# The last two hidden chunks of each MLP stage share one accumulation per token tile

## What is computed

```python
def swiglu(h, w_gu, w_down):
    g, u = jnp.split(h @ w_gu, 2, axis=-1)
    return (jax.nn.silu(g) * u) @ w_down

def _sq_relu_mlp(h, w1, w2):
    return jnp.square(jax.nn.relu(h @ w1)) @ w2

def sandwich(x, fn, g_pre, g_post, shift, scale, gate, res_w):
    h = modulate(rmsnorm(x, g_pre), shift, scale)
    y = rmsnorm(fn(h), g_post)
    return x + res_w * gate[:, None, :] * y
...
    x = sandwich(x, ffn1, ...)      # 2816 hidden columns
    x = sandwich(x, mix, ...)
    x = sandwich(x, ffn2, ...)      # 2816 hidden columns
...
        x = x + gx1 * _rms_norm(_token_mixer(h, kv_ctx, rope, lp, lam, lam_init), g_post_mix[l])
        hm = _modulate(x, g_pre_mlp[l], sx2, cx2)
        x = x + gx2 * _rms_norm(_sq_relu_mlp(hm, w_ff1[l], w_ff2[l]), g_post_mlp[l])   # 4096 hidden columns
```

## Time and profile before

| | us |
|---|---|
| runs (3) | 4396.05, 4403.17, 4407.77 |
| median | 4403.17 |
| the profiled execution | 4407.63 |
| its span | 4405.6 |

### The profile page before, as it was taken

How to read it: one execution, slowest core, us unless ns; L and a number is a source line. 1 busy time by engine, 2 the same in 40 slices (tenths; PEclk the granted TensorE clock), 3 DMA queues, 4 the chain that set the end, 5 groups by cost and what they waited for, 6 DMA issues and landing times.

```text
span 4405.6 us, 50811 instructions
## 1 busy us (share of the span) xinstructions
PE 3956.6 (90%) x18628; PEld 3175.8 (72%) x18628; DVE 2291.0 (52%) x3495; ACT 1369.2 (31%) x1832; POOL 1346.1 (31%) x1012
## 2 busy tenths in 40 slices
PE   7999899989997979789879879999787989788999
PEld 6888676867776748558668768888674747577887
DVE  4676844146664361641682367777445353834334
ACT  3222633242224242252112331111424243225223
POOL 2444332434432103003222223322220303434443
PEclk8999999999998989899989989999998999899999
DMA  4454221233331102001111123332110201222222
GB/s 180 176 190 156 85 72 63 96 115 128 137 132 49 39 0 72 20 1 58 57 58 58 58 82 125 118 119 100 45 48 10 82 1 67 77 84 79 95 95 86
DMA packets 57219, 364.66 MB, mean 83 GB/s; under 512 B 5744, under 2 KB 12144, under 8 KB 13936
## 3 DMA queue, kind: packets, MB, share of 16 engines
q1 hardware_dynamic: 42064, 271.11, 17.5%
q10 hardware_dynamic: 15008, 91.49, 5.5%
HBM read 360.49 MB, written 2.10 MB: 82 GB/s over the span
## 4 chain that ended last, share of the span: by engine, by line
issue 66%; POOL 23%; PE 10%; DVE 0%; ACT 0%; POOLq 0%; DVEq 0%; ACTq 0%
POOL b_wlo L561 23%; PE ps L1647 3%; PE ps L1648 3%; PE ps L1649 3%; POOLq L575 0%; ACT ps L616 0%; DVE b_y L1156 0%; DVE b_x L1160 0%; PE ps L1699 0%; DVE b_y L1183 0%; PE ps L1710 0%; ACT b_whi L602 0%; POOLq L577 0%; DVE b_y L1209 0%; PE ps L1723 0%
## 5 line engine op out<-in xcount | busy, mean ns | idle before, releaser
L561 POOL TENSOR_TENSOR b_wlo<-b_raw,b_whi 128x512 fp32r<-128x512 f32 x1008 | 1345.9, 1366 | 3039.1 <-ACT b_whi L602 3039.1
L1647 PE MATMUL ps<-b_hhi,b_whi 128*128 128x512 f32 (+1 forms) x3160 | 1178.5, 373 | 69.5 <-DVE b_vp L1548 28.8
L1648 PE MATMUL ps<-b_hlo,b_whi 128*128 128x512 f32 (+1 forms) x3160 | 1163.3, 368 | 0.0
L1649 PE MATMUL ps<-b_hhi,b_wlo 128*128 128x512 f32 (+1 forms) x3160 | 1161.4, 368 | 0.0
L1647 PEld LDWEIGHTS ps<-b_hhi,b_whi 128*128 128x128 f32 x3160 | 603.5, 191 | 177.2 <-issue 57.3
L602 ACT ACTIVATE b_whi<-b_raw 128x2048 fp32r<-128x2048 f32 x252 | 480.7, 1908 | 752.4 <-PE ps L1649 744.9
L1648 PEld LDWEIGHTS ps<-b_hlo,b_whi 128*128 128x128 f32 x3160 | 603.7, 191 | 97.8 <-issue 2.2
L1649 PEld LDWEIGHTS ps<-b_hhi,b_wlo 128*128 128x128 f32 x3160 | 602.2, 191 | 99.1
L1104 DVE SCALAR_TENSOR_TENSOR b_macc<-b_mraw,b_csil,b_macc 128x256 f32<-128x256 f32 x868 | 506.0, 639 | 7.0
L1209 DVE TENSOR_TENSOR b_y<-ps,b_y 128x512 f32<-128x512 f32 x496 | 335.8, 689 | 274.7 <-PE ps L1649 274.7
L1647 PE MATMUL ps<-b_whi,b_dhi 128*128 128x512 f32 x992 | 399.7, 403 | 53.5 <-POOL b_wlo L561 29.0
(11 more groups left out here) (277 smaller groups left out, 4752.0 us busy)
## 6 DMA issues: line engine op xcount, KB each, us to landing
b_raw<-panels SPq DMA_DIRECT2D x252, 1024.0 KB, 4.8
b_mraw<-mod_panels ACTq DMA_DIRECT2D x78, 1024.0 KB, 6.7
b_y<-mod_panels ACTq DMA_DIRECT2D x3, 1024.0 KB, 15.9
b_xin<-xT SPq DMA_DIRECT2D x1, 2048.0 KB, 25.5
b_mraw<-mod_panels SPq DMA_DIRECT2D x2, 1024.0 KB, 19.0
b_rope<-rope ACTq DMA_DIRECT2D x4, 512.0 KB, 3.9
outT<-b_xout SPq DMA_DIRECT2D x4, 512.0 KB, 3.8
b_mod<-mod_panels ACTq DMA_DIRECT2D x1, 1024.0 KB, 20.9
```

Of the source, the lines that this page charges most:

```text
L561: ins = pool.tensor_tensor(wlo[:, s, c], raw[:, s, c], whi[:, s, c].bitcast(F32), ALU.subtract)
L1647: pe.matmul(out, a[0], b[0], start=first, stop=False)
L1648: pe.matmul(out, a[0], b[1], start=False, stop=False)
L1649: return pe.matmul(out, a[1], b[0], start=False, stop=last)
```

## The change

`last_downs` takes the place of the last two rounds. It makes the parts of chunk C-2 for output tiles 0, 1 and 2, then the modulation sums of the last chunk, and then, for every output tile, the part of chunk C-1 into the same bank without clearing it (from tile 3 on preceded by the part of chunk C-2). DVE adds each tile once. The last chunk's work leaves the loop (ffn1 and ffn2 run one trip less and have one chunk more ahead of it); the number of modulation sums per chunk stays. D0 and D1 are both released only in the last output tile. N0 is split after the root of the last post step, where N1 was; N1 after the last pre root, ahead of the norm's tail. The low part of a padding panel at the very end is dropped.

```diff
-    MLPS = {"ffn1": Mlp("ffn1", True, L, first["ffn1"], 8, ((2, 2), 3, 4)),
-            "ffn2": Mlp("ffn2", True, L, first["ffn2"], 36, ((), 2, 5)),
+    MLPS = {"ffn1": Mlp("ffn1", True, L, first["ffn1"], 8, ((2, 2, 3), 3, 3, (3,))),
+            "ffn2": Mlp("ffn2", True, L, first["ffn2"], 36, ((2,), 2, 4, (2,))),
...
-            upto = next_panel(st) + 1 if st in NEXT else n_panels
+            upto = next_panel(st) + 1 if st in NEXT else MLPS["mlp2"].p0 + 2 * MLPS["mlp2"].C
...
                     if t == last and pre:
-                        split(next_panel(st) + 1)
+                        split(next_panel(st))
+                        if finish:
+                            split(next_panel(st) + 1)
...
+            if pre:
+                split(next_panel(st) + 1)
             norm_tail(st)
...
-            split(m.p0 + m.UP * m.C + m.C)
             gate_rows(AFTER[st], (0, 1, 2, 3))
...
             for c in m.rest:
-                units(c)
-                for o in range(O):
-                    add(c - 1, o)
+                units(c, mods=m.rest_mods(c))
+                if c < m.C - 1:
+                    for o in range(O):
+                        add(c - 1, o)
             prepare(AFTER[st])
             def finish(t):
-                add(m.C - 1, 2 * t)
-                add(m.C - 1, 2 * t + 1)
+                add(m.C - 2, 2 * t)
+                add(m.C - 2, 2 * t + 1)
...
+            def last_downs():
+                p, c = m.panel(m.C - 1) + m.UP, m.C - 2
+                def part(o, n):
+                    tok, half = slice(o // 2 * P, (o // 2 + 1) * P), o % 2
+                    if n == 0:
+                        prior = O * (c + 1) + o - 3 if o >= 3 else O * c + max(q for q in range(O) if q % 3 == o)
+                        pe.wait_ge(*at("added", ("start", st), prior + 1))
+                    for k in range(2):
+                        ins = tri(ps[:, 4 + o % 3, :], (dhi[:, (c + n) % 2, k, tok], dlo[:, (c + n) % 2, k, tok]),
+                                  wtile(p + n, 2, D, k, half * 512, 512), n == k == 0, n == k == 1)
+                    if o == O - 1:
+                        ins.then_inc(panel_used, 1)
+                    elif n == 1:
+                        ins.then_inc(*up("down"))
+                pe.wait_ge(lo_ready, p + 1)
+                pe.wait_ge(*at("hid_lo", ("start", st), 2 * c + 2))
+                for o in range(3):
+                    part(o, 0)
+                sums(m.rest_mods(m.C - 1))
+                pe.wait_ge(lo_ready, p + 2)
+                pe.wait_ge(*at("hid_lo", ("start", st), 2 * c + 4))
+                for o in range(O):
+                    if o >= 3:
+                        part(o, 0)
+                    part(o, 1)
+                    if o == 1:
+                        gate_rows(AFTER[st], (0, 1, 2, 3))
...
-            down(m.C - 1, m.p0 + (m.UP + 1) * m.C - 1)
+            last_downs()
```

More of the change, by code:

```diff
@@ L233, in __init__ @@
         self.O = 2 * T // P
-        self.lead, self.half, self.trips = mods
+        self.lead, self.half, self.trips, self.tail = mods
         self.loop0 = 1 + len(self.lead)
         self.rest = range(self.loop0 + 2 * self.trips, self.C)
+        assert len(self.tail) == len(self.rest) >= 1
         self.per_trip = 2 * (self.UP + 1)
@@ L251, in loop_mods, with rest_mods @@
         return self.mod0 + sum(self.lead) + u * self.half, self.half
+    def rest_mods(self, c):
+        n = c - self.rest[0]
+        return self.mod0 + sum(self.lead) + 2 * self.trips * self.half + sum(self.tail[:n]), self.tail[n]
 class Rows:
@@ L461, in program @@
     first = {**{n: 10 ** 6 for n in ("mix1", "ffn2", "mix2", "mlp1", "mix3", "mlp2")}, **first}
-    MLPS = {"ffn1": Mlp("ffn1", True, L, first["ffn1"], 8, ((2, 2), 3, 4)),
-            "ffn2": Mlp("ffn2", True, L, first["ffn2"], 36, ((), 2, 5)),
-            "mlp1": Mlp("mlp1", False, TT, first["mlp1"], 56, ((), 2, 7)),
-            "mlp2": Mlp("mlp2", False, L, first["mlp2"], 84, ((), 0, 7))}
+    MLPS = {"ffn1": Mlp("ffn1", True, L, first["ffn1"], 8, ((2, 2, 3), 3, 3, (3,))),
+            "ffn2": Mlp("ffn2", True, L, first["ffn2"], 36, ((2,), 2, 4, (2,))),
+            "mlp1": Mlp("mlp1", False, TT, first["mlp1"], 56, ((), 2, 7, (0,))),
+            "mlp2": Mlp("mlp2", False, L, first["mlp2"], 84, ((), 0, 7, (0,)))}
     LAYER, TOKENS = {"mix2": 0, "mix3": 1}, {"mix2": TT, "mix3": L}
@@ L708, in mlp @@
             for c in m.rest:
-                units(c, m.panel(c))
+                units(c, m.panel(c), mods=m.rest_mods(c))
                 split(m.panel(c) + m.UP + 1)
-            split(m.p0 + m.UP * m.C + m.C)
             gate_rows(AFTER[st], (0, 1, 2, 3))
@@ L1205, in add @@
                 else:
-                    dve.wait_ge(panel_used, lin(down_panel(m, c) + 1, m.per_trip, i))
+                    dve.wait_ge(panel_used, lin(down_panel(m, c if c < m.C - 2 else m.C - 1) + 1, m.per_trip, i))
                 dve.wait_ge(*at("added", ("start", st), lin(O * c + o + 1, 2 * O, i)))
@@ L1790, in down @@
                         ins.then_inc(*up("down"))
-                    if c == m.C - 1 and o == 1:
+                ins.then_inc(panel_used, 1)
[10 more added lines that the diff above has]
+                    if o == O - 1:
+                        ins.then_inc(panel_used, 1)
+                    elif n == 1:
[12 more added lines that the diff above has]
+                    if o == 1:
                         gate_rows(AFTER[st], (0, 1, 2, 3))
-                ins.then_inc(panel_used, 1)
-            first_ups()
             def sums(mods, i=None):
@@ L1799, in sums @@
                     mod(mods[0] + v, i, 2 * m.half)
+            first_ups()
             for n in range(len(m.lead)):
@@ L1812, in mlp @@
                 ups(c, m.panel(c))
-                down(c - 1, m.panel(c) + m.UP)
-            down(m.C - 1, m.p0 + (m.UP + 1) * m.C - 1)
+                if c < m.C - 1:
+                    down(c - 1, m.panel(c) + m.UP)
+                    sums(m.rest_mods(c))
+            last_downs()
         free = {}
```

## The result

The changed kernel takes 4419.1 us in the median (4415.02 to 4420.06, 9 runs), the kernel before in the same sessions 4407.77 us. The ratio is 1.0027 with an interval of 1.0017 to 1.0038: it is slower by about 12 us, 7 to 17. The profiled execution has a span of 4415.2 us against 4405.6, +9.6. The forecast had been +8.7, and 4411.9 us for the median. The measured median lies 7.2 us above that; 4.6 us of these are the base, since nine runs of the kernel before give 4407.77 where the first three gave 4403.17.

The account below looks back on a forecast made before the run. TensorE, busy 90% of the span, was taken as the bound, so DVE work pays only at four seams. Terms 3.3 - 2.1 + 0.8 + 4.9 + 1.8 gave +8.7 us, median 4403.2 to 4411.9, range 4400 to 4422.

Parts of the forecast that it names:

- What is removed: 36 adds, 25 us of DVE, worth something only at seams; last add then ends 0.7 us after last part.
- The wait for D1: After three parts and the sums TensorE waits for D1's low part, 4.4 us in ffn1, since its split does not move.
- n3: Seam from ffn2's end into its norm: no wait for D1, last add at 1354.8 against 1356.9, -2.1 us.
- The clock: TensorE's granted clock falls to about half behind a wait of 4.4 to 5.6 us, costing 2.0 us, bounds 0 and 3.4.
- Rival 1: Clock does not fall after the new waits; three seams lose 2.0 us less, median 4405.9, chance 0.15.
- rival 2: Some 10 us at half clock behind each of three new waits, 5.0 instead of 2.0 each; 4420.9, chance 0.12.
- n1: Seam from ffn1's end into its norm: last add at 452.5 against 449.2, +3.3 us.
- n5: Seam from mlp1's end into its norm: wait 5.6, last add at 3149.4 against 3148.6, +0.8 us.
- n7: Seam at mlp2's end: wait 4.9, last add at 4398.8 against 4393.9, +4.9 us.
- N0 and N1: N1's POOL quarters now fall on DVE's `hlo` steps, 0.6 us at each seam but the last, +1.8 us.
- rival 3: N0 comes late and N1's split delays the first `hhi`; three seams lose some 2 us more, 4417.9, chance 0.07.
- Rival 4: D1 is not late, so only DVE's relief is left; 21 us off the forecast, 4391, chance 0.04.

Follow-up runs that it names:

- unfused_gates: Kernel before, two rounds of down products and all adds kept, only the gate rows made ahead of the last round; 4411.79 us, ratio 1.0006.
- split_only: Kernel before with only the splits of the next stage's panels moved, as in the change; 4408.04 us, ratio 1.0004.
- filler: Changed kernel plus 60 useless matmuls ahead of the wait for D1 in ffn1, mlp1 and mlp2; 4410.56 us, ratio 1.0008.
- no_wait: Changed kernel, last chunk's down products read D0 instead of D1, so TensorE need not wait and the result is incomplete; 4395.6 us, ratio 0.9973.
- gates_five: Changed kernel with gate rows and, in 512-token stages, five parts of C-2 instead of three ahead of D1's wait; 4387.35 us, ratio 0.9955.

## Why the prediction was right, step by step

**What is removed.** Right. The last add follows the last part by 0.7 us, at every seam, and the adds elsewhere brought nothing: between the seams nothing is shorter beyond what repeats differ by; those stretches are 1.5 us longer in all.

**The wait for D1.** 4.4, 0, 5.6 and 4.9 us were forecast, 4.0, 1.2, 5.4 and 4.8 measured. The first is 0.4 us shorter because something did move: ACT starts the last hidden values of ffn1, and D1's split behind them, 1.8 us after its first copy, where it was 2.2 us before (why is not shown).

n3's term was mis-sized: -2.1 forecast, -0.9 measured. I had let the half clock behind the 1.8 us wait, seen in the earlier trace rows, stand at the start of ffn2's parts. In this execution it did not come; TensorE was 1.7 us earlier at the sums, met D1's late low part there, waited 1.2 us, and the half clock came behind that wait. One short wait was taken for a fixed price of 1.7 us, where it is paid at one time and not at another. Even the gain of 0.9 us hangs on this. Of three profiles of kernels without the fused sums, two have the half clock at that place (the kernel before and unfused_gates) and one has not (split_only); of seven with the fused sums none has it. Against split_only's n3 of 51.7 us, where neither side has the half clock at that place, the change loses 0.8 us in n3 instead of gaining 0.9. That the sign came out as forecast was luck with the clock; whether the change itself makes the half clock rarer there is not shown.

**The clock.** 2.0 us per wait forecast; 2.8, 1.9 and 2.2 read from the stretches, together 6.9, of which the filler brought back 5.7 to 6.0 in the seams. Rival 1 (no half clock) and rival 2 (some 10 us of it) are both excluded: the stretches were 5.6, 3.8 and 4.4 us long.

**The four terms.** n1 +3.3 forecast, +3.5 measured; n5 +0.8 and +0.4; n7 +4.9 and +5.0; n3 see above. The four seams by forecast +6.9, measured +8.1.

**N0 and N1.** +1.8 forecast, hardly anything measured. The `hlo` rows are longer as supposed, but TensorE's first up product comes only 0 to 0.4 us later than in the kernel before, counted from the first `hlo`, and split_only shows no loss. The step that failed is the price for each seam: I had only bounded it from rows of a norm in which DVE is the bound, and here TensorE is. N0 was not late (rival 3).

**Unrolled chunks.** Priced at 0; the stretch from mix1's start to ffn2's last ups, with the longer unrolled code, is 855.3 us after and 855.6 before. Up to ffn1's last ups the program is 0.9 us longer than before, but unfused_gates, which unrolls nothing, is 1.2 us longer there, so this says nothing of the unrolling.

**Rival 4.** Its state of things was made by no_wait: 22.6 us less than the changed kernel by the medians where 21 was the figure. The 21 were for three seams, which gained 21; n3, priced at nothing, gave 3.1 to 3.4 more in the seams. Rival 4 had been judged out of reach as nothing in ACT's or POOL's order moves. That was true of the change, but the other side can move: work of TensorE placed ahead of the wait does the same, and gates_five went below it.

Errors of 1 to 2 us cancelled: n3 (+1.2), `hlo` (-1.8) and the stretches between the seams (+1.5, priced at 0). So it is partly luck that the total of 8.7 is so near the 9.6 of the span. The median moved by 11.3 us with an interval of 7 to 17; whether the 1.7 us between this and the span are real can't be told.

## What to carry to other kernels

When products are joined into one accumulation, the second operand is needed earlier than before; count the work that stands between the two, for the buffers may have a rule that makes the second operand late by a fixed time. Fewer adds are worth nothing where their engine waits anyway; at the seams, where it was behind, the gain came only when the work that others wait for (gate rows) and spare PSUM banks filled the gap. Price a wait of TensorE with the clock behind it: here some 2 us on top of each wait of 4 to 5.

## What the runs showed of the hardware

Extra matmuls can shorten a program: 60 of them, about 13.7 us of work, in place of waits of 4.0 to 5.4 us brought 7.6 us by the medians, 5.7 to 6.0 us by the seams. A wait of the same length does not always lower the clock. TensorE waits some 1.8 us for POOL nine times in ffn2, before and after alike, and the clock falls to half behind five of these waits in the kernel before and behind four in the changed one; these two stretches (kernel before, TensorE) follow two such waits one chunk apart, and only the second is at half clock:

```profile
1243.80:1247.20 3.40, 3.40 (x15) 1.00 0.67 217
1281.40:1284.80 3.40, 3.40 (x10) 0.50 0.95 311
```

A whole untouched stretch (mix2 and mlp1's chunks) was 1734 to 1735 us long in eight of the ten profiles, 1731 in one and 1729 in one. Spans of single executions therefore decide nothing under some 6 us here. The seams are steadier: in the two profiles of the changed kernel each repeats within 0.4 us, their sum within 0.6; but n3 can differ by the 1.7 us of the clock.
